# The opening of a two-block forward pass: modulation by matmul on four column groups, x loaded first, projections by halves

## The chip, the cores and the metric

The kernel runs on one core of one Trainium2 chip. The metric is device time in microseconds (us) for one launch; the kernel before takes 1517.32 us, the median of three runs (1516.11 to 1517.71). All data are fp32.

## The reference

The whole program is two transformer-like blocks on 512 tokens of width 1024. This case touches the start of the first one:

```python
mod_l = (silu(c)     @ w_mod + b_mod)[:, None, :]    # w_mod 1024 x 6144; 6 parts of 1024
mod_c =  silu(c_ctx) @ w_mod + b_mod                 # only csh1 and csc1 are used
sh1, sc1, g1, sh2, sc2, g2 = split(mod_l, 6)
csh1, csc1, ...            = split(mod_c, 6)
h  = rms(x,   norm1_g) * (1 + sc1)  + sh1            # 512 tokens
hc = rms(ctx, norm1_g) * (1 + csc1) + csh1           # 256 context tokens
p, pc = h @ w_in, hc @ w_in                          # q (384), kv (256), k_pe (32), f (512), ga, gb (1024 each)
# then: low-rank q, k, v, attention of 8 heads, a Fourier branch, the merge with w_out,
# 16 experts, and a second block (recurrent unit, short convolution, feed-forward)
```

## The kernel before

Everything is stored with channels on the 128 partitions. x is eight tiles of 128 channels by 512 tokens (`x0`), ctx eight tiles by 256 tokens (`c0`). The projections are done at better than single-pass precision: a weight and an activation are each split into a rounded part and a remainder (`w_hi`, `w_lo`, `h_hi`, `h_lo`) and each product is three matmuls (`mm3`, L817 to L819). One weight block is 128 x 128 values, and its three matmuls stream 512 tokens (256 for ctx).

**The weight stream.** All weights come in chunks of 128 x 2048 values (1 MB) through a ring of four slots, `raw`. SP (SyncE) issues the loads in the order of `CHUNKS`, and each refill waits until the chunk four places earlier has been used. A chunk that is to be split is rounded on ACT (L1392, `w_hi`) and its remainder is taken on POOL (L746, `w_lo`); there are three slots of these. A chunk of w_mod is used directly. Before, the first eight chunks are those of sc1 and sh1 (`mod_a`), then come the chunks of `s1` (w_in and others), and the 16 chunks of the other four parts of w_mod (`mod_b`) stand behind chunks 9 to 17 of `s1`.

**The first modulation** (`mod_a`, before). Each chunk has two tiles of 128 outputs. The first tile is done on PE with the weights stationary and the two columns of silu(c), silu(c_ctx) moving (L842). The second tile is done by DVE for c (L1754, L1756: a product and seven multiply-adds of 128 x 128, `macc_x`) and by POOL for c_ctx (L783, L765), and PE sums these over partitions with a column of ones (L847). `mod_evac` (L1706) adds the bias.

**The norm.** ACT squares x and ctx (L1416, L1417), DVE sums the eight tiles (L1768), PE sums over partitions (L866, `columns`), DVE takes the inverse square root by Newton steps (L1734 to L1746), PE spreads the result over partitions (L873, `broadcast`). Then for each tile j: DVE multiplies (`pre`, L1794), ACT adds the shift and rounds (`h_hi`, L1402), DVE takes the remainder (`h_lo`, L1801), in two buffers. PE projects `cq` 0 and 1 together as the tiles of h appear, then `cq` 2, `ckv`, `kpe`, and then `f` 0 (the first tile of the Fourier branch), the sums of squares `ssq_c`, `f` 1, and so on.

**The order** on each engine is written out by hand. A plan (`make_plan`) gives each PSUM tile a bank, says what frees it, and counts the tiles (`tile_full`), by which ACT knows when to split the next weight chunk and SP when a chunk has been used.

**The second modulation** (`mod_b`, L1721 and L1723) runs on DVE beside PE's projections `ga`, `gb` and `four_o`: for each of 16 chunks a product and seven multiply-adds of 128 x 256 elements into `macc` in SBUF. PE sums each over partitions (L856), and between them DVE evacuates `four_o` (L1923, `gbf`).

## Time and profile before

| | us |
|---|---|
| median of three runs | 1517.32 |
| the profiled execution | 1515.58 |
| its span | 1513.8 |
| PE busy in the span | 1412.9 (93%) |
| DVE busy | 747.3 (49%) |
| first projection matmul starts | 81.85 |
| `f` 0 starts | 125.06 |

The profile page gives the busy time of each engine over the span and in 40 slices, the chain of work that ended last, and the costliest groups of instructions. Its slices show PE at 4 to 5 tenths in the first two, and at 9 nearly everywhere later. In a timeline row the columns are start, length, engine, line, operation, output and inputs, shape and count; what stands in brackets is the idle time before it and what ended that. On PE an fp32 matmul has two rows. PE rows overlap: what counts is the spacing of their starts.

### The profile page before, as it was taken

How to read it: one execution, taken by the hardware profiler on the slowest of the kernel's cores; microseconds unless marked ns; L12 is line 12 of the kernel's file. 1: busy time of each engine (PE TensorE's matmuls, PEld its weight loads, DVE VectorE, ACT ScalarE, POOL GpSimd, SP SyncE). 2: the span in 40 equal slices, each digit the busy share in tenths (PEclk: the TensorE clock that was granted, in tenths of full speed). 3: DMA queues.
4: the chain of work that ended last, by engine and by line, in shares of the span. 5: the costliest groups of instructions: out<-in, count | busy, mean ns of one | idle time of the engine just before them, and what ended most of it. 6: DMA issues, size and time to landing. Idle time of an engine off the chain costs nothing.

```text
span 1513.8 us, 15775 instructions
## 1 busy us (share of the span) xinstructions
PE 1412.9 (93%) x6456; PEld 1056.9 (70%) x6456; DVE 747.3 (49%) x1245; ACT 445.7 (29%) x563; POOL 423.6 (28%) x127
## 2 busy tenths in 40 slices
PE   5599999998999977999998999999999999999997
PEld 5478887775667874444443767877888888888886
DVE  7962479976567144333323475571145154352442
ACT  1141332224654131110001346332234143232330
POOL 6531233330211210000001322543424434344340
PEclk9998999998999968999999999999999999999998
DMA  7241116650012423999998311322213322223201
GB/s 275 108 167 56 57 56 255 247 221 0 30 54 84 167 111 147 397 385 399 399 396 343 116 56 56 111 87 80 84 63 132 111 84 94 83 102 111 84 1 56
DMA packets 31908, 221.96 MB, mean 147 GB/s; under 512 B 3776, under 2 KB 4416, under 8 KB 5472
## 3 DMA queue, kind: packets, MB, share of 16 engines
q1 hardware_dynamic: 30400, 215.77, 37.3%
q10 hardware_dynamic: 1440, 5.24, 0.9%
q8 instruction: 48, 0.79, 0.2%
q14 instruction: 20, 0.16, 0.0%
HBM read 218.90 MB, written 2.10 MB: 146 GB/s over the span
## 4 chain that ended last, share of the span: by engine, by line
PE 79%; DVE 17%; issue 1%; ACT 1%; DMA 1%; POOL 0%; DVEq 0%; SPq 0%; ACTq 0%
PE psum L817 18%; PE psum L818 18%; PE psum L819 18%; PE psum L1196 12%; DVE macc L1723 5%; DVE macc_x L1756 3%; PE psum L1068 2%; PE psum L866 2%; PE psum L1181 2%; PE psum L1156 1%; PE psum L1157 1%; DMA raw<-in_stream 1%; PE psum L1043 1%; PE psum L1125 1%; PE psum L1184 1%
## 5 line engine op out<-in xcount | busy, mean ns | idle before, releaser
L746 POOL TENSOR_TENSOR w_lo<-raw,w_hi 128x2048 fp32r<-128x2048 f32 x82 | 378.5, 4618 | 974.2 <-ACT w_hi L1392 699.6
L817 PE MATMUL psum<-b_hi,w_hi 128*128 128x512 f32 x608 | 239.8, 394 | 2.4 <-DVE conv_u L2171 1.3
L819 PE MATMUL psum<-b_hi,w_lo 128*128 128x512 f32 x608 | 236.7, 389 | 0.0
L818 PE MATMUL psum<-b_lo,w_hi 128*128 128x512 f32 x608 | 236.6, 389 | 0.0
L1392 ACT ACTIVATE w_hi<-raw 128x2048 fp32r<-128x2048 f32 x82 | 156.2, 1907 | 232.4 <-DMA raw<-in_stream 116.4
L817 PEld LDWEIGHTS psum<-b_hi,w_hi 128*128 128x128 f32 x608 | 114.2, 188 | 28.2 <-DVE conv_u L2171 2.2
L818 PEld LDWEIGHTS psum<-b_lo,w_hi 128*128 128x128 f32 x608 | 114.2, 188 | 24.2 <-issue 1.2
L819 PEld LDWEIGHTS psum<-b_hi,w_lo 128*128 128x128 f32 x608 | 114.1, 188 | 24.0
L1196 PE MATMUL psum<-ex,xe 128*64 128x512 f32 x512 | 122.3, 602 | 0.7 <-ACT xe L1574 0.7
L2015 DVE SCALAR_TENSOR_TENSOR x<-psum,mod,x 128x512 f32<-128x512 f32 x72 | 53.9, 750 | 128.4 <-PE psum L1184 91.0
L2013 DVE TENSOR_TENSOR x<-psum,x 128x512 f32<-128x512 f32 x40 | 27.6, 692 | 159.9 <-PE psum L819 159.9
L817 PE MATMUL psum<-h_hi,w_hi 128*128 128x512 f32 (+1 forms) x208 | 84.0, 404 | 5.0 <-DVE h_lo L1801 1.8
L1723 DVE SCALAR_TENSOR_TENSOR macc<-raw,small,macc 128x256 f32<-128x256 f32 x112 | 84.1, 751 | 4.0
L818 PE MATMUL psum<-h_lo,w_hi 128*128 128x512 f32 (+1 forms) x208 | 82.3, 396 | 0.0
L819 PE MATMUL psum<-h_hi,w_lo 128*128 128x512 f32 (+1 forms) x208 | 82.3, 396 | 0.0
L1196 PEld LDWEIGHTS psum<-ex,xe 128*64 128x64 f32 x512 | 32.2, 136 | 62.1 <-issue 61.3
L817 PE MATMUL psum<-ff_hi,w_hi 128*128 128x512 f32 x192 | 75.3, 392 | 0.0
L819 PE MATMUL psum<-ff_hi,w_lo 128*128 128x512 f32 x192 | 74.8, 389 | 0.0
L818 PE MATMUL psum<-ff_lo,w_hi 128*128 128x512 f32 x192 | 74.7, 389 | 0.0
L2242 DVE TENSOR_TENSOR psum<-psum,rstd_s 128x512 f32<-128x512 f32 x48 | 33.5, 697 | 77.4 <-PE psum L819 77.4
L1196 PE MATMUL psum<-ex,act_e 128*64 128x512 f32 x256 | 58.4, 610 | 1.6 <-DVE act_e L2142 1.6
L817 PEld LDWEIGHTS psum<-h_hi,w_hi 128*128 128x128 f32 (+1 forms) x208 | 39.3, 189 | 15.8 <-issue 2.9
(352 smaller groups left out, 2422.4 us busy)
## 6 DMA issues: line engine op xcount, KB each, us to landing
raw<-in_stream SPq DMA_DIRECT2D x106, 1024.0 KB, 4.9
ex<-in_stream SPq DMA_DIRECT2D x96, 1024.0 KB, 8.9
x<-in_x SPq DMA_DIRECT2D x1, 2048.0 KB, 15.4
x<-in_x ACTq DMA_DIRECT2D x1, 2048.0 KB, 7.4
out<-y_out ACTq DMA_DIRECT2D x8, 256.0 KB, 2.2
c<-in_ctx SPq DMA_DIRECT2D x1, 1024.0 KB, 17.5
wab<-in_wab ACTq DMA_DIRECT2D x1, 1024.0 KB, 6.7
cols<-in_cols SPq DMA_DIRECT2D x1, 166.5 KB, 2.3
```

The lines of the kernel that those rows point to most:

```text
L746: nc.gpsimd.tensor_tensor(w_lo[:, slot, :], raw[:, raw_slot, :], w_hi[:, slot, :].bitcast(F32), ALU.subtract).then_inc(w_lo_done, 1)
L817: mm(o, w[0], x[0], start=start, stop=False)
L818: mm(o, w[0], x[1], start=False, stop=False)
L819: return mm(o, w[1], x[0], start=False, stop=stop)
L866: last = mm(o[:, at + t:at + t + 1], src[:, t * P:(t + 1) * P], one[0:rows, :], start=start and t == 0, stop=stop, skip_group_check=True)
L1068: return mm(psum[:, 6 + h % 2, :], va, probs[:, k % 3, :], start=k == 0, stop=k == KT - 1)
L1196: last = mm(o[e * CAP:(e + 1) * CAP, :], x_of(k, e), w[:, (2 * (k - k0) + e) * T:(2 * (k - k0) + e + 1) * T], start=k == 0, stop=k == ks - 1)
L1392: A(w_hi[:, c % NHL, :], raw[:, n % NRAW, :], ACT.Copy).then_inc(w_hi_done, 1)
L1723: ins = V.scalar_tensor_tensor(out=acc, in0=w[:, :, k, :], scalar=csil[:, 2 * k:2 * k + 1], in1=acc, op0=ALU.mult, op1=ALU.add)
L1756: ins = V.scalar_tensor_tensor(out=macc_x[:, c, :], in0=w, scalar=s, in1=macc_x[:, c, :], op0=ALU.mult, op1=ALU.add)
L2015: ins = V.scalar_tensor_tensor(out=x1[:, j, :], in0=o, scalar=scale, in1=x1[:, j, :], op0=ALU.mult, op1=ALU.add)
L2242: V.tensor_tensor(o, o, rstd, ALU.mult).then_inc(ffz_done, 1)
```

## The change

1. **Order of loads.** cols, then x in four pieces of two tiles each with semaphores of their own, ident, then the ring. The stream is now: chunk 0 of `s1`, two chunks of w_mod, chunk 1 of `s1`, six chunks of w_mod, chunk 2 of `s1`. ctx is loaded just ahead of ring chunk 10.
2. **First modulation.** The chunks of w_mod are laid out by rows: each holds four blocks of 128 inputs by 512 outputs. They are now the moving operand, and silu(c), silu(c_ctx), padded with zeros to 32 columns (`cpad`), the stationary one. The four blocks go to four groups of 32 columns of the array and so to four groups of 32 partitions of one PSUM bank, two chunks summed in each. ACT copies the 128 x 512 result to SBUF (`mod_rows`), and four small matmuls with a 0/1 matrix (`sel`) sum the four groups and turn the result back to channels on partitions (`mod_tile`). The four tiles hold the first half of sc1, the first half of sh1, the second half of sc1, the second half of sh1. DVE's and POOL's part in it is gone.
3. **Norm of x.** PE sums the squares of all eight tiles itself (`ssq_x`, 32 small matmuls); the norm of ctx has its own tile (`ssq_cc`) and Newton steps, and its squares and DVE sum stand between the halves.
4. **Projections by halves.** The five tiles `cq` 0 to 2 and `ckv` 0, 1 of x are open together. For h tiles 0 to 3 all five take each tile as it comes, with modulation tiles 2 and 3 between them; then each of the five takes h tiles 4 to 7. The weight blocks are laid out to match: chunk 0 has `cq` for tiles 0 to 3, chunk 1 has `ckv`, chunk 2 `cq` for tiles 4 to 7, `kpe` and the start of `f`.
5. **Second modulation.** The accumulator lies in PSUM bank 7; only the last multiply-add writes `macc` in SBUF.

```diff
+MOD_M0 = (8, 0, 12, 4)
+MOD_BEHIND = {0: 2, 1: 6, 9: 1, 10: 2, 11: 2, 12: 2, 13: 2, 14: 2, 15: 2, 16: 2, 17: 1}
...
+    p.add("ssq_x", by=("rcol_done", 1), bank=5)
     for g in range(4):
-        if g == 3:
-            p.add("ssq_xc", by=("rcol_done", 1))
-        p.add("mod", g, raw=(2 * g, 2 * g + 1))
-    p.add("bc_x", by=("pre_done", KD))
-    p.add("bc_c", by=("pre_done", 2 * KD))
+        p.add("rows", g, by="act", raw=(2 * g, 2 * g + 1), bank=6)
+        if g == 0:
+            p.add("bc_x", by=("pre_done", KD), bank=5)
+        p.add("mod", g, bank=7)
+    p.add("ssq_cc", by=("rcol_done", 2), bank=6)
     for j in range(QL):
-        p.add("cq", j, split=blocks(s1, S1_QKV + j * 8 * B, 8))
+        p.add("cq", j, split=(s1, s1 + 2), bank=j)
+    p.add("bc_c", by=("pre_done", 2 * KD), bank=7)
     for j in range(KL):
-        p.add("ckv", j, 0)
-        p.add("ckv", j, 1, split=blocks(s1, S1_QKV + (QL + j) * 8 * B, 8))
-    p.add("kpe", 0)
+        p.add("ckv", j, 0, split=(s1 + 1,), bank=QL + j)
+    p.add("kpe", 0, split=blocks(s1, S1_KPE, 2), bank=5)
...
+            for i in range(4):
+                sp.dma_start(x0[:, 2 * i:2 * i + 2, :], x_d[:, 2 * i:2 * i + 2, :]).then_inc(x_in[i], 16)
+            sp.dma_start(ident[:], ident_d).then_inc(ident_in, 16)
             for n in range(NRAW):
                 load(n, n)
-            sp.dma_start(x0[:], x_d).then_inc(x_in, 16)
-            sp.dma_start(c0[:], ctx_d).then_inc(x_in, 16)
-            sp.dma_start(ident[:], ident_d).then_inc(consts_in, 16)
...
+                if n == 10:
+                    sp.dma_start(c0[:], ctx_d).then_inc(ctx_in, 16)
                 refill(n)
...
+            def mod_rows_tile(g):
+                o = open_tile("rows", g)
+                for c in range(2):
+                    w = raw_chunk(RAW_OF_RAW[2 * g + c])
+                    for i in range(4):
+                        last = mm(o[32 * i:32 * i + 32, :], cpad[:, 4 * c + i, :], w[:, i * T:(i + 1) * T],
+                                  start=c == 0, stop=c == 1)
+                done(last)
...
                 o = open_tile("mod", g)
-                for c in range(2):
-                    w = raw_chunk(2 * g + c)
-                    for k in range(KD):
-                        mm(o[:, 4 * c:4 * c + 2], w[:, k * B:(k + 1) * B], csil[:, 2 * k:2 * k + 2],
-                           start=k == 0 and c == 0, stop=k == KD - 1, skip_group_check=True)
-                for c in range(2):
-                    for i, (acc, ready) in enumerate(((macc_x, macc_x_done), (macc_c, macc_c_done))):
-                        pe.wait_ge(ready, 2 * g + c + 1)
-                        last = mm(o[:, 4 * c + 2 + i:4 * c + 3 + i], acc[:, 2 * g + c, :], one, start=False, stop=True,
-                                  skip_group_check=True)
+                pe.wait_ge(freed_act, PLAN.freed_count(TILE["rows", g]))
+                for b in range(4):
+                    last = mm(o[:, 2 * b:2 * b + 2], mod_rows[:, g % 2, b * P:(b + 1) * P], col("sel", 0, 2),
+                              start=True, stop=True)
                 done(last)
...
+            o = open_tile("ssq_x")
+            for j in range(KD):
+                pe.wait_ge(sq_done, j // 2 + 1)
+                last = columns(o, 0, sq_x0[:, j, :], TT, start=j == 0, stop=j == KD - 1)
+            done(last)
             pe.wait_ge(silu_done, 1)
-            for g in range(4):
-                if g == 3:
-                    o = open_tile("ssq_xc")
-                    pe.wait_ge(sum_done, 1)
-                    columns(o, 0, sum_x, TT)
-                    pe.wait_ge(sum_done, 2)
-                    done(columns(o, TT, sum_c, 2, start=False))
-                mod_tile(g)
-            pe.wait_ge(consts_in, 16 * 7)
-            o, o2 = open_tile("bc_x"), open_tile("bc_c")
+            mod_rows_tile(0)
+            pe.wait_ge(ident_in, 16)
+            o = open_tile("bc_x")
             wait_rcol()
             done(broadcast(o, 0, TT))
-            done(broadcast(o2, TT, 2))
+            mod_tile(0)
+            mod_rows_tile(1)
+            mod_tile(1)
...
+            for k in range(4):
+                for i in range(QL + KL):
+                    qkv_step(i, k)
+                if k == 0:
+                    mod_rows_tile(2)
+                if k == 1:
+                    mod_tile(2)
+                    mod_rows_tile(3)
+                if k == 2:
+                    mod_tile(3)
+            o = open_tile("ssq_cc")
+            pe.wait_ge(sum_done, 1)
+            done(columns(o, 0, sum_c, 2))
+            for i in range(QL + KL):
+                if i == QL:
+                    o = open_tile("bc_c")
+                    wait_rcol()
+                    done(broadcast(o, 0, 2))
+                for k in range(4, KD):
+                    last = qkv_step(i, k)
+                done(last)
+            pe.wait_ge(consts_in, 16 * 6)
...
+            def rows_copy(g):
+                o = take("rows", g)
+                if g >= 2:
+                    full(act, "mod", g - 2)
+                A(mod_rows[:, g % 2, :], o, ACT.Copy).then_inc(freed_act, 1)
+            def h_hi_part(j):
+                hi_of_pre(h_hi[:, j, :], pre[:, j % 2, :], bias=mod[:, j, 0:1])
+            rows_copy(0)
+            rows_copy(1)
+            for j in range(2):
+                h_hi_part(j)
+            rows_copy(2)
+            for j in range(2, 4):
+                h_hi_part(j)
+            rows_copy(3)
+            act.wait_ge(ctx_in, 16)
             A(sq_c0[:], c0[:], ACT.Square).then_inc(sq_done, 1)
-            act.wait_ge(consts_in, 16 * 7)
-            A(dftc_hi[:], dftc[:], ACT.Copy).then_inc(act_seq, 1)
-            for g in range(4):
-                split_weights(TILE["mod", g])
-            for j in range(KD):
-                hi_of_pre(h_hi[:, j, :], pre[:, j % 2, :], bias=mod[:, j, 0:1])
+            for j in range(4, KD):
+                h_hi_part(j)
             for j in range(KD):
                 hi_of_pre(hc_hi[:, j, :], pre[:, j % 2, 0:TC], bias=mod[:, j, 1:2])
+            act.wait_ge(consts_in, 16 * 6)
+            A(dftc_hi[:], dftc[:], ACT.Copy).then_inc(act_seq, 1)
...
                 dve.wait_ge(raw_full[n % NRAW], 16 * (n // NRAW + 1))
+                if c < 2:
+                    dve.wait_ge(qtok_done, 2 * TT)
+                else:
+                    dve.wait_ge(macc_done, c - 1)
                 w = raw[:, n % NRAW, :].rearrange("p (m k c) -> p m k c", m=2, k=KD)
-                acc = macc[:, c % 4, :, :]
+                acc = psum[:, 7, c % 2 * 2 * B:(c % 2 + 1) * 2 * B].rearrange("p (m c) -> p m c", m=2)
                 link(V.tensor_scalar(acc, w[:, :, 0, :], csil[:, 0:1], None, ALU.mult))
                 for k in range(1, KD):
-                    ins = V.scalar_tensor_tensor(out=acc, in0=w[:, :, k, :], scalar=csil[:, 2 * k:2 * k + 1], in1=acc,
-                                                 op0=ALU.mult, op1=ALU.add)
+                    ins = V.scalar_tensor_tensor(out=acc if k < KD - 1 else macc[:, c % 4, :, :], in0=w[:, :, k, :],
+                                                 scalar=csil[:, 2 * k:2 * k + 1], in1=acc, op0=ALU.mult, op1=ALU.add)
...
+            inverse_norms(take("ssq_x"), 4, [(0, 4, 1.0 / D)])
+            mod_evac(0)
+            gains(0)
+            mod_evac(1)
+            norm(4, mk0(x0, a1, take("bc_x"), "h"), lo0(h_lo, h_hi, 0, "h", T))
+            dve.wait_ge(sq_done, 5)
+            V.tensor_reduce(sum_c[:], sq_c0[:].rearrange("p k t -> p t k"), AX.X, ALU.add).then_inc(sum_done, 1)
+            mod_evac(2)
+            gains(1)
+            mod_evac(3)
+            norm(KD, mk0(x0, a1, bank("bc_x"), "h"), lo0(h_lo, h_hi, 0, "h", T), 4)
+            inverse_norms(take("ssq_cc"), 2, [(0, 2, 1.0 / D)])
+            norm(KD, mk0(c0, a1c, take("bc_c")[:, 0:TC], "hc"), lo0(hc_lo, hc_hi, 1, "hc", TC))
```

How the instructions move on PE at the start (before; `macc_x` and `macc_c` are the partial products of DVE and POOL, `small` holds the norms):

```order
L842 MATMUL psum<-small,raw 128x2 x16
L847 MATMUL psum<-ones,macc_x 128x1
L847 MATMUL psum<-ones,macc_c 128x1
...
L866 MATMUL psum<-ones,sum_x 128x1 x4
L866 MATMUL psum<-ones,sum_c 128x1 x2
L842 MATMUL psum<-small,raw 128x2 x16
...
L873 MATMUL psum<-ident,small 128x128 x6
L817 MATMUL psum<-h_hi,w_hi 128x512
```

and after:

```order
L854 MATMUL psum<-ones,sq_x_67 128x1 x32
L826 MATMUL psum<-raw,cpad 32x512 x8
L861 MATMUL psum<-ident,small 128x128 x4
L835 MATMUL psum<-cols,mod_rows 128x2 x4
L826 MATMUL psum<-raw,cpad 32x512 x8
L835 MATMUL psum<-cols,mod_rows 128x2 x4
L802 MATMUL psum<-h_hi,w_hi 128x512
```

The first projection now stands behind two of the four modulation tiles; the other two (L826, L835) stand behind the projections of h tiles 0, 1 and 2.

On ACT, after the change, from the squares of x to the shift of the last tile of h (`w_hi` is the splitting of weight chunks):

```order
L1433 ACTIVATE sq_x_67<-x_65 128x1024 x4
L1406 ACTIVATE w_hi<-raw 128x2048 x2
L1440 ACTIVATE mod_rows<-psum 128x512 x2
L1416 ACTIVATE h_hi<-pre,mod 128x512 x2
L1440 ACTIVATE mod_rows<-psum 128x512
L1416 ACTIVATE h_hi<-pre,mod 128x512 x2
L1406 ACTIVATE w_hi<-raw 128x2048
L1440 ACTIVATE mod_rows<-psum 128x512
L1454 ACTIVATE sq_c_68<-c_66 128x2048
L1416 ACTIVATE h_hi<-pre,mod 128x512 x4
```

Before, both squares stood ahead of the two `w_hi`, and nothing stood between the eight `h_hi`; now the third weight chunk, the copy of a modulation tile and the squares of ctx stand in their middle.

On DVE, after the change, between tile 3 and tile 4 of h:

```order
L1810 SCALAR_TENSOR_TENSOR h_lo<-pre,mod,h_hi 128x512 x2
L1825 TENSOR_REDUCE sum_c<-sq_c_68 128x256
L1743 TENSOR_TENSOR mod<-psum,cols 128x8
L1816 SCALAR_TENSOR_TENSOR small<-mod,cols 128x4 x2
L1743 TENSOR_TENSOR mod<-psum,cols 128x8
L1803 SCALAR_TENSOR_TENSOR pre<-x_65,small,psum 128x512 x2
```

The sum of the squares of ctx now stands ahead of the evacuation of modulation tile 2, which frees the bank of modulation tile 3.

## Rows read from the trace of the kernel before

**Rows 1.** Busy time by stretch: length; PE, PEld, DVE, ACT, POOL busy; PEclk; DMA share, GB/s.

```profile
0.00:81.80 81.80, 41.16 (x184) 40.07 (x184) 69.13 (x90) 12.42 (x9) 44.23 (x39) 1.00 0.52 200
81.80:125.00 43.20, 43.15 (x216) 34.84 (x217) 21.43 (x37) 17.73 (x25) 13.82 (x3) 1.00 0.33 127
205.00:335.00 130.00, 123.77 (x564) 101.59 (x563) 117.18 (x215) 30.00 (x31) 46.72 (x10) 0.99 0.56 212
280.00:285.00 5.00, 5.00 (x16) 3.92 (x16) 4.82 (x6) 2.40 (x2) 2.89 (x1) 0.66 0.87 351
```

**Rows 2.** The chain that ended last, 0 to 84 us: shares by line.

```profile
by line: DVE macc_x L1756 54.7%; issue 9.8%; DVE macc_x L1754 9.1%; DMA raw<-in_stream 6.1%; DVE sum_c L1768 4.4%; PE psum L873 2.5%; PE psum L847 2.4%; PE psum L817 1.4%; DVE sum_x L1768 1.4%; PE psum L818 1.0%; DVE h_lo L1801 0.9%; DVE pr
```

**Rows 3.** Timeline, the start: loads and what waited for them.

```profile
3.28 0.47 SPq L694 DMA_DIRECT2D x<-in_x  x1
6.41 2.02 DVE L1754 TENSOR_SCALAR macc_x<-raw,small 128x128 f32<-128x128 f32 x1 [5.54 <-DMA raw<-in_stream]
21.28 3.62 ACT L1416 ACTIVATE sq_x<-x 128x4096 f32<-128x4096 f32 x1 [17.99 <-DMA c<-in_ctx]
```

**Rows 4.** DMA issues of the page: KB each, us to landing.

```profile
raw<-in_stream SPq DMA_DIRECT2D x106, 1024.0 KB, 4.9
```

**Rows 5.** Timeline: small matmuls and Newton's end, start of the span to 80 us.

```profile
36.11 6.96 PE L842 MATMUL psum<-small,raw 128*128 128x2 f32 x32
77.14 2.90 PE L873 MATMUL psum<-ident,small 128*128 128x128 f32 x12 [1.40 <-DVE mod L1706]
```

**Rows 6.** Timeline: expert matmuls, two groups of 64 columns, moving 512 columns.

```profile
606.96 5.37 PE L1196 MATMUL psum<-ex,act_e 128*64 128x512 f32 x24
```

**Rows 7.** Timeline of PE: the first projections, later ones, and ctx, kpe and f.

```profile
81.85 0.76 PE L817 MATMUL psum<-h_hi,w_hi 128*128 128x512 f32 x1 [1.81 <-DVE h_lo L1801]
82.83 0.63 PE L819 MATMUL psum<-h_hi,w_lo 128*128 128x512 f32 x1
83.26 0.63 PE L817 MATMUL psum<-h_hi,w_hi 128*128 128x512 f32 x1
...
105.14 0.39 PE L818 MATMUL psum<-h_lo,w_hi 128*128 128x512 f32 x1
105.36 0.39 PE L819 MATMUL psum<-h_hi,w_lo 128*128 128x512 f32 x1
...
116.68 0.28 PE L819 MATMUL psum<-hc_hi,w_lo 128*128 128x256 f32 x1
116.80 0.39 PE L817 MATMUL psum<-h_hi,w_hi 128*32 128x512 f32 x1
117.03 0.39 PE L818 MATMUL psum<-h_lo,w_hi 128*32 128x512 f32 x1
...
125.06 0.40 PE L817 MATMUL psum<-h_hi,w_hi 128*128 128x512 f32 x1
```

**Rows 8.** Timeline: weight splitting, the sum of ctx, steps of h.

```profile
58.29 1.91 ACT L1392 ACTIVATE w_hi<-raw 128x2048 fp32r<-128x2048 f32 x1 [31.28 <-DMA raw<-in_stream]
58.37 3.72 DVE L1768 TENSOR_REDUCE sum_c<-sq_c 128x256 f32<-128x2048 f32 x1
60.27 9.01 POOL L746 TENSOR_TENSOR w_lo<-raw,w_hi 128x2048 fp32r<-128x2048 f32 x2 [9.70 <-ACT w_hi L1392]
83.85 0.72 ACT L1402 ACTIVATE h_hi<-pre,mod 128x512 fp32r<-128x512 f32 x1 [0.72 <-DVE pre L1794]
85.18 0.75 DVE L1801 SCALAR_TENSOR_TENSOR h_lo<-pre,mod,h_hi 128x512 fp32r<-128x512 f32 x1
```

**Rows 9.** Second modulation on DVE, with POOL working (230 to 239) and not (226).

```profile
226.81 3.61 DVE L1723 SCALAR_TENSOR_TENSOR macc<-raw,small,macc 128x256 f32<-128x256 f32 x7
230.72 7.82 DVE L1723 SCALAR_TENSOR_TENSOR macc<-raw,small,macc 128x256 f32<-128x256 f32 x7
233.45 4.81 POOL L746 TENSOR_TENSOR w_lo<-raw,w_hi 128x2048 fp32r<-128x2048 f32 x1 [16.00 <-ACT w_hi L1392]
```

**Rows 10.** DVE and POOL around 309 us.

```profile
308.35 4.61 POOL L746 TENSOR_TENSOR w_lo<-raw,w_hi 128x2048 fp32r<-128x2048 f32 x1 [8.79 <-ACT w_hi L1392]
308.85 0.69 DVE L1923 TENSOR_TENSOR gbf<-psum,sg 128x512 f32<-128x512 f32 x1 [2.88 <-ACT sg L1470]
309.52 3.58 DVE L1721 TENSOR_SCALAR macc<-raw,small 128x256 f32<-128x256 f32 x1
```

More of the change, by code:

```diff
@@ L155, in raw_chunks @@
             if name == "s1":
-                for _ in range(MODB_BEHIND.get(c, 0)):
+                for _ in range(MOD_BEHIND.get(c, 0)):
                     add(False)
@@ L1432, in _ @@
                 square(sq_q[:, j, :], take("cq", j))
-            for j in range(KL):
-                square(sq_kv[:, j, 0:T], take("ckv", j, 0))
-                square(sq_kv[:, j, T:TK], take("ckv", j, 1)[:, 0:TC])
-            A(sqk[NOPE:QK, 0:T], take("kpe", 0)[0:ROPE, :], ACT.Square).then_inc(act_seq, 1)
-            A(sqk[NOPE:QK, T:TK], take("kpe", 1)[0:ROPE, 0:TC], ACT.Square).then_inc(act_seq, 1)
+            for s in range(2):
+                w = slice(T, TK) if s else slice(0, T)
+                n = TC if s else T
+                for j in range(KL):
+                    square(sq_kv[:, j, w], take("ckv", j, s)[:, 0:n])
+                A(sqk[NOPE:QK, w], take("kpe", s)[0:ROPE, 0:n], ACT.Square).then_inc(act_seq, 1)
             hi(f_hi[:, 0, :], take("f", 0))
@@ L1704, in mod_evac @@
             def mod_evac(g):
-                b = cols[:, COLS["b_mod"] + 4 * g:COLS["b_mod"] + 4 * g + 4].unsqueeze(2).to_broadcast([P, 4, 2])
-                free(V.tensor_tensor(mod[:, 4 * g:4 * g + 4, :], take("mod", g)[:, 0:8].rearrange("p (m c) -> p m c", c=2),
+                m = MOD_M0[g]
+                b = col("b_mod", m, 4).unsqueeze(2).to_broadcast([P, 4, 2])
+                free(V.tensor_tensor(mod[:, m:m + 4, :], take("mod", g)[:, 0:8].rearrange("p (m c) -> p m c", c=2),
                                      b, ALU.add))
@@ L1803, in lo0, with gains @@
                 return f
-            norm(KD, None, mk0(x0, a1, take("bc_x"), "h"), lo0(h_lo, h_hi, 0, "h", T))
-            norm(KD, None, mk0(c0, a1c, take("bc_c")[:, 0:TC], "hc"), lo0(hc_lo, hc_hi, 1, "hc", TC))
-            nsq = 2
+            def gains(half):
+                for i, a in ((0, a1), (1, a1c)):
+                    link(V.scalar_tensor_tensor(out=a[:, 4 * half:4 * half + 4], in0=mod[:, KD + 4 * half:KD + 4 * half + 4, i],
+                                                scalar=1.0, in1=col("norm1_g", 4 * half, 4), op0=ALU.add, op1=ALU.mult))
+            inverse_norms(take("ssq_x"), 4, [(0, 4, 1.0 / D)])
[11 more added lines that the diff above has]
+            norm(KD, mk0(c0, a1c, take("bc_c")[:, 0:TC], "hc"), lo0(hc_lo, hc_hi, 1, "hc", TC))
+            dve.wait_ge(act_seq, 1)
+            link(V.tensor_tensor(dftc_lo[:], dftc[:], dftc_hi[:].bitcast(F32), ALU.subtract))
+            nsq = 5
             for j in range(QL):
@@ L2322 @@
     w_mod = a["w_mod"][0]
-    mod = tiles(w_mod)
+    rows_a = [w_mod[(4 * c + i) * P:(4 * c + i + 1) * P, m * P:m * P + T] for m in MOD_M0 for c in range(2) for i in range(4)]
+    mod = np.concatenate(rows_a + [tiles(w_mod)[:, 8 * CH:]], axis=1)
     w_in = a["w_in"][0]
```

143 lines of the change are left out of this document (52 added, 91 removed), and 2 rows, old and new, of the table _n.

## The prediction

> **What bounds the kernel now.** I read the busy time by stretch first. PE is busy 41 of the first 81.8 us and practically all of the next 43 [rows 1]; the page has it at nine tenths nearly everywhere after. So what ends PE's early waits shortens the program, and what is done beside PE later is free. The chain of waits says who sets the opening: 54.7% of it is DVE's multiply-add for the first modulation, 9.1% its product, and 4.4% the sum of ctx's squares [rows 2]. PE's first projection starts at 81.85, released by the first tile of h, and `f` 0, which both kernels reach with the same work done, starts at 125.06 [rows 7]. Between 205 and 335 us PE is idle 130 − 123.8 = 6.2 us, and in one stretch of 5 us its granted clock is 0.66 [rows 1], 1.7 us more; this is the stretch of the second modulation, on a DVE busy 117 of 130 us. The reader is to see two places only: the start, and this one.
>
> **The opening, step by step.** *Loads.* The first ring chunk is there at 6.41, after cols and itself (1.2 MB); ctx, the last large load, at 21.3 after 7.5 MB [rows 3]. That is 6.3 MB in 14.9 us, 0.42 MB a us, 2.5 us a chunk. With x first: first piece of x near 5, all of x at 8.9, then chunk 0 of `s1` 11.5, two of w_mod 14.0 and 16.5, chunk 1 of `s1` 19.0.
>
> *PE, squares of x.* `ssq_x` is 32 small matmuls, 64 rows. 32 rows of small matmuls (moving 2 columns) took 6.96 us in the same opening [rows 5], so 13.9 us: from 6.2 (one ACT square after the first piece) to 20.1. This is new on PE and now sets the start; Newton's steps and `bc_x` lie beside or just behind it.
>
> *Rows tiles.* The trace has no matmul on four groups of 32 columns. The nearest row is the experts': two groups of 64 columns, 512 moving, 24 rows in 5.37 us [rows 6], so 0.224 a row; two matmuls side by side are four rows, 0.9 us. One alone would be 0.9 as well if the pair is really side by side. Bounds for a chunk of four: 0.9 us (all side by side) and 3.6 (one after the other). I take 0.9, since the experts' rows show groups overlapping. The first projections start 0.43 us apart (82.83, 83.26) and later ones 0.22 [rows 7]: after the opening's small matmuls and waits PE works at the lower of its two clock levels (1.2 against 2.4 GHz), though the page's granted clock stands at 1.00. I take the slow rate for this opening too: 1.7 us a chunk. Rows tile 0: 20.1 to 23.5. `bc_x` is 8 rows of the kind of which 12 took 2.90 [rows 5], 1.9 us, and modulation tile 0 8 rows at 0.22, 1.7 us: to 27.2.
>
> *The ring.* The second chunk of rows tile 1 takes the slot of the first w_mod chunk, so it is loaded when rows tile 0 is done, 23.5, and lands 4.9 us later [rows 4] at 28.4. Its matmuls end at 30.1, ACT's copy (like `h_hi`, 0.72 [rows 8]) at 30.8, modulation tile 1 at 32.6, its evacuation at 32.8, and from `pre` to the first projection the chain before needs 2.5 us (`pre`, `h_hi`, `h_lo`; 0.75, 0.72, 0.75 [rows 8]). First projection at 35.4 instead of 81.85: 46.4 us earlier.
>
> *From there to `f` 0.* The projections are the same matmuls, 43.2 us before (125.06 − 81.85, the slow start included). Added on PE: rows tiles 2 and 3 at the full clock, 3.6; modulation tiles 2 and 3, 2.9; `ssq_cc` 0.6 and `bc_c` 1.0. Then a new wait. PE reaches modulation tile 3 at 35.4 + 5.0 + 1.8 + 3.4 + 1.2 + 1.8 + 3.4 = 52.0 (three groups of 15 matmuls, the rows tiles, tile 2). Its bank is freed by DVE's evacuation of tile 2, queued behind the sum of ctx's squares, 3.72 us [rows 8], which waits for ACT's square (1.9 us), which stands behind the third weight chunk: loaded at 42.2 when rows tile 2 is done, landed 47.1, split by ACT in 1.91 [rows 8]. That gives copy 49.7, square 51.6, sum 55.3, evacuation 55.5: PE waits 3.5 us. The row of 280 to 285 us shows the clock granted at 0.66 after a wait of this size [rows 1], so I add 1.7 us. At tile 7 of h PE is ahead of DVE by 1.2 us. Sum of what is added: 3.6 + 2.9 + 1.6 + 3.5 + 1.7 + 1.2 = 14.5. `f` 0 starts at 35.4 + 43.2 + 14.5 = 93.1, **32.0 us earlier**.
>
> *Covers.* The norm of ctx (8 steps on DVE, under 8 us) ends near 81, its matmuls start near 84; weight chunk 3 is split by ACT and POOL (1.91 and 4.6 us [rows 8]) by 90, `f` 0 needs it at 93. Each has some 3 us; if one fails, the wait is a few us.
>
> A rule that speaks against the change: the Trainium skill (TensorEngine Tiling, Key Properties) says that changing the tiling mode drains TensorE, and the rows tiles change it eight times. The trace goes from 128 to 32 output columns at 116.68 and the next rows start 0.12 and 0.23 us on [rows 7], no later than within one mode. By the row the sum stands; what a drain would cost is a rival below.
>
> **The second modulation.** A chunk's seven multiply-adds take DVE 3.61 us, or 7.82 when POOL splits a weight chunk beside them [rows 9]: one of them lasts as long as POOL's. Ten POOL operations fall in this stretch [rows 1], each worth 4.2 us of DVE. A DVE operation with one input in PSUM ran through POOL's at 0.69 us (308.85), while a product with only SBUF operands, 0.6 us later, was held for 3.58 [rows 10]. With the accumulator in PSUM the multiply-adds are of the first kind: 16 chunks at 3.9 us are 63 us instead of about 100, and PE's projections (5.4 us and more for each) set the pace. What PE can get back is 6.2 + 1.7 = 7.9 us. Bounds: 0 (POOL holds the new form too, or PE finds another wait) and 7.9. I take **7.0**, since nearly all of PE's waits there hang on DVE or on the ring that DVE feeds.
>
> The first operation of a chunk has one SBUF input and writes PSUM, and no row shows that form. By the row at 309.52 it can be held; the Trainium skill (VectorE: DVE Perf Modes, Mode 2×_2P) has the held mode only with source and destination both in SBUF, so it would never be. It is one operation in eight, so the sum goes by the rest either way.
>
> After 335 us nothing is moved: the same waits come 39 us earlier.
>
> **Sum.** The profiled execution took 1515.58 us: 1515.6 − 32.0 − 7.0 = 1476.6. The median of the three runs is 1.7 above it, so 1478.3, **1478 us**.
>
> **Rivals.**
> - *Column groups one after the other.* For: no row shows four. Against: the experts' pairs overlap [rows 6]. Rows tile 0 would cost 13.4 instead of 3.4 (eight at 1.68), the second chunk of rows tile 1 5 more, tiles 2 and 3 5.4 more each: 26 us, so 1504.
> - *The second modulation gives nothing*, by either bound above: 1485.
> - *PE's clock is high in the opening.* Small matmuls at half the time: `ssq_x` 7 us less, though the ring then holds rows tile 1 for a while; no slow stretch after the wait: 8 us less in all, 1470. Against: 6.96 us of small matmuls in a row did not speed up [rows 5].
> - *Each change between 128 and 32 columns stops PE.* Eight changes (into and out of four rows tiles), each at most as long as one slow fp32 matmul, 1.7 us: 13 us, 1491. Against: the spacing at 116.68 [rows 7]. This is the case of the Trainium skill's rule above (TensorEngine Tiling).
> - *The gain is lost altogether* by a wait in the coupled queues (ring, ACT, DVE, PE in order) that I have missed: 1517. It would need 39 us in a stretch of 90.
> - *Slower: the accumulator in PSUM makes DVE the bound.* Place: the 16 chunks, DVE from 222 to 326 us before. It decides when a chunk takes more than (326 + 32 − 222 − 5)/16 = 8.2 us, that is 1.0 us an operation instead of 0.5. At 1.5 us the chunks end near 222 + 192 + 5 = 419, 93 us later than now, less 32: 1578. Against: 0.69 us for 512 elements with PSUM input [rows 10]; these have 256.
>
> **Chances.** Forecast 0.62; groups in turn 0.12; stops at mode changes 0.03; no gain in the second modulation 0.09; high clock 0.10; all lost 0.02; slower 0.02. A difference under 0.2%, 3 us, can't be told from none. Faster 0.96, the same 0.02, slower 0.02. Range 1469 to 1497: the high-clock case and a few single misses (a cover of 3 us gone, the slow clock kept longer, part of the groups in turn) are in it, the full 26 us and the last two are not.
>
> **What would show it.** Right: `f` 0 near 93 us, first projection near 35; `ssq_x` about 14 us; a rows tile 2 us or less when dense; PE waiting 3 to 4 us for DVE in the middle of the halves; no multiply-add over 1 us beside POOL's; PE idle under 2 us in the stretch of `ga`, `gb`, `four_o`. Wrong: rows tiles of 7 us; a multiply-add held by POOL; `ctx` or weight chunk 3 releasing PE late.

## The result and the profile after

The changed kernel takes 1473.18 us (median of four runs, 1472.33 to 1475.54) where the kernel before took 1516.71 beside it: ratio 0.9721 [0.9698, 0.9744]. The forecast was 1478 with a range of 1469 to 1497. Run again later, with the kernel before beside it once more, it took 1474.46 (five runs) against 1516.45, ratio 0.9728 [0.9708, 0.9748]. Its profiled execution took 1472.33 us with a span of 1470.5: 43.3 us under that of before, where the prediction's sum said 39.0.

First the busy time by stretch, with the columns of [rows 1]; the first two lines end at the first projection and at `f` 0, the third is the stretch of the second modulation, the rest are short looks at the clock.

```profile
0.00:35.40 35.40, 22.97 (x120) 18.11 (x120) 6.29 (x20) 12.22 (x13) 9.70 (x8) 0.95 0.92 338
35.40:91.50 56.10, 53.13 (x272) 40.54 (x273) 28.18 (x55) 20.53 (x29) 9.45 (x3) 0.91 0.41 155
171.50:297.00 125.50, 124.41 (x577) 103.08 (x577) 89.89 (x215) 31.65 (x32) 46.07 (x10) 1.00 0.60 226
...
55.00:61.00 6.00, 5.69 (x18) 4.82 (x19) 4.30 (x10) 2.00 (x3) 0.00 (x0) 0.55 0.51 201
61.00:64.00 3.00, 3.00 (x14) 2.50 (x13) 2.64 (x7) 0.84 (x2) 0.00 (x0) 0.77 0.00 0
```

PE was idle 40.6 us before the first projection and is now idle 12.4. In the third stretch it was idle 6.2 of 130 us and is now idle 1.1 of 125.5.

The chain that ended last, 0 to 92 us, shares by line, answers to [rows 2]:

```profile
by line: PE psum L854 15.3%; PE psum L802 15.0%; PE psum L803 14.1%; PE psum L804 13.8%; DMA raw<-in_stream 10.4%; PE psum L826 7.2%; DMA x<-in_x 5.2%; DVE sum_c L1825 4.0%; PE psum L835 3.4%; issue 2.8%; ACT sq_c L1454 2.0%; ACT mod_rows L
```

DVE's multiply-adds, 54.7% of it before, are gone; the squares on PE (L854) are the largest line, and a tenth is the ring.

The timeline of PE and of what it waits for, from the squares of x to `f` 0:

```profile
7.14 13.78 PE L854 MATMUL psum<-ones,sq_x 128*128 128x1 f32 x64 [7.14 <-ACT sq_x L1433]
20.86 3.64 PE L826 MATMUL psum<-raw,cpad 128*32 128x512 f32 x16
24.43 1.35 PE L861 MATMUL psum<-ident,small 128*128 128x128 f32 x8
25.61 0.95 PE L835 MATMUL psum<-cols,mod_rows 128*128 128x2 f32 x8
26.49 1.06 PE L826 MATMUL psum<-raw,cpad 128*32 128x512 f32 x8
29.41 1.06 PE L826 MATMUL psum<-raw,cpad 128*32 128x512 f32 x8 [1.86 <-DMA raw<-in_stream]
31.29 1.49 PE L835 MATMUL psum<-cols,mod_rows 128*128 128x2 f32 x8 [0.81 <-ACT mod_rows L1440]
35.44 0.79 PE L802 MATMUL psum<-h_hi,w_hi 128*128 128x512 f32 x1 [2.66 <-DVE h_lo L1810]
...
40.48 1.92 PE L826 MATMUL psum<-raw,cpad 128*32 128x512 f32 x16
42.33 0.50 PE L802 MATMUL psum<-h_hi,w_hi 128*128 128x512 f32 x1
...
51.50 3.68 DVE L1825 TENSOR_REDUCE sum_c<-sq_c 128x256 f32<-128x2048 f32 x1 [6.37 <-ACT sq_c L1454]
55.31 1.66 PE L835 MATMUL psum<-cols,mod_rows 128*128 128x2 f32 x8 [2.94 <-DVE mod L1743]
...
91.53 0.40 PE L802 MATMUL psum<-h_hi,w_hi 128*128 128x512 f32 x1
```

These answer to [rows 5] and [rows 7]. The first projection stands at 35.44 (81.85 before), `f` 0 at 91.53 (125.06): 33.5 us earlier. The sum of ctx's squares runs from 51.50 to 55.18, and PE waits behind it.

Two executions of one and the same opening are not alike. The opening of before, unchanged in the first experiment below, starts its projections at 81.85 in one trace and at 77.97 in the other, and `f` 0 at 125.06 and 122.08. The changed opening, up to its first projection the same in four traces of this record, starts them between 34.64 and 36.56, and in the three of them that are the same up to `f` 0 this stands between 90.42 and 93.06. No run shows what makes this scatter. A difference of two single traces carries some 3 us of it.

The summary of DVE's operations of the second modulation (shortest, median, longest duration in ns; first and last start), first before, then after, answers to [rows 9]:

```profile
L1723 DVE SCALAR_TENSOR_TENSOR macc<-raw,small,macc x112: 483/485/4940, 222.9 to 325.1; 128x256 f32<-128x256 f32 x112
```

```profile
L1764 DVE SCALAR_TENSOR_TENSOR psum<-raw,small,psum x96: 487/490/493, 189.0 to 276.1; 128x256 f32<-128x256 f32 x96
L1764 DVE SCALAR_TENSOR_TENSOR macc<-raw,small,psum x16: 481/481/482, 192.1 to 276.6; 128x256 f32<-128x256 f32 x16
L1762 DVE TENSOR_SCALAR psum<-raw,small x16: 475/486/489, 188.4 to 272.9; 128x256 f32<-128x256 f32 x16
```

The longest fell from 4940 to 493 ns: none is held beside POOL any more, though POOL works as long as before (46.07 us in the stretch, 46.72 before). The 16 products and 112 multiply-adds together take DVE 62.5 us instead of 92.9; the prediction had 63 and about 100.

Where the 43.3 us came from, by the start of the same work in both traces: `f` 0 33.5 us earlier, the transposes of q behind the second modulation 42.0 (350.6 and 308.6), the first expert matmul 41.0, the last matmul of the feed-forward 43.2. So in this pair of traces the opening gave 33.5 and the stretch with the second modulation 8.5; everything later changed the distance by at most 2.2 us.

### The profile page after: what moved, and what is told of

Same layout as the page of the kernel before. It is cut to its first block, busy times and chain, and to the rows that moved or that the text cites. A ratio compares the mean times of both kernels' runs of the same rounds, so it can differ in the third digit from the quotient of the medians.

```text
span 1470.5 us, 15704 instructions
## 1 busy us (share of the span) xinstructions
PE 1400.3 (95%) x6448; PEld 1039.3 (71%) x6448; DVE 661.9 (45%) x1194; ACT 448.9 (31%) x571; POOL 388.8 (26%) x96
## 4 chain that ended last, share of the span: by engine, by line
PE 88%; DVE 8%; ACT 1%; DMA 1%; issue 1%; POOL 0%; DVEq 0%; SPq 0%; ACTq 0%
PE psum L802 20%; PE psum L804 20%; PE psum L803 20%; PE psum L1210 12%; PE psum L854 3%; PE psum L1082 2%; PE psum L1195 2%; PE psum L1170 1%; PE psum L1171 1%; PE psum L1057 1%; DMA raw<-in_stream 1%; PE psum L1139 1%; PE psum L1198 1%; PE psum L1269 1%; PE psum L861 1%
## 5 line engine op out<-in xcount | busy, mean ns | idle before, releaser
L803 PEld LDWEIGHTS psum<-b_lo,w_hi 128*128 128x128 f32 x608 | 114.2, 188 | 24.5 <-issue 1.2
L802 PE MATMUL psum<-h_hi,w_hi 128*128 128x512 f32 (+1 forms) x208 | 85.3, 410 | 3.7 <-DVE h_lo L1810 2.7
L2267 DVE TENSOR_TENSOR psum<-psum,rstd_s 128x512 f32<-128x512 f32 x48 | 33.5, 698 | 77.4 <-PE psum L804 77.4
L1764 DVE SCALAR_TENSOR_TENSOR psum<-raw,small,psum 128x256 f32<-128x256 f32 x96 | 47.0, 490 | 3.4
```

The source lines that it names most:

```text
L802: mm(o, w[0], x[0], start=start, stop=False)
L803: mm(o, w[0], x[1], start=False, stop=False)
L1764: ins = V.scalar_tensor_tensor(out=acc if k < KD - 1 else macc[:, c % 4, :, :], in0=w[:, :, k, :], scalar=csil[:, 2 * k:2 * k + 1], in1=ac ...
L2267: V.tensor_tensor(o, o, rstd, ALU.mult).then_inc(ffz_done, 1)
```

## The experiments

Each starts from the kernel named; the cuts show the lines that matter. `f` 0 is its start in the profiled execution. The experiments ran in groups, each with the kernel before beside it, whose median was between 1513.58 and 1516.71 us. Ratios to it are the safer comparison between groups.

**Which part gives what.** The kernel before with the accumulator in PSUM alone:

```diff
-acc = macc[:, c % 4, :, :]
+acc = psum[:, 7, c % 2 * 2 * B:(c % 2 + 1) * 2 * B]...     # the last multiply-add still writes macc
```

The waits for the bank, which the diff of the change shows, come with it.

> The kernel before, with only the second modulation's accumulator moved to PSUM bank 7; the opening is the old one. Theory: POOL's weight splitting holds a DVE operation with two SBUF inputs and not one with an input in PSUM, and this alone gives what the changed kernel gained behind f 0, about 8.5 us: 1508 us (1506 to 1511), every multiply-add near 0.49 us, PE idle under 2 us between 205 and 335 us and no fall of its clock there. Rival: that stretch gained because the opening shifted the ring of weights against POOL; PSUM alone gives 0 to 3 us: 1514 to 1517.

Measured: 1506.35 us (8 runs; before 1513.58, 13 runs), ratio 0.9945 [0.9925, 0.9965], 7.2 us by the medians: as the theory said, and outside the rival's 1514 to 1517. The stretch of [rows 1]:

```profile
205.00:335.00 130.00, 129.24 (x599) 107.18 (x598) 93.74 (x225) 35.48 (x39) 46.07 (x10) 1.00 0.55 210
```

PE's idle time is 0.8 us instead of 6.2, and no slow clock is left. From `f` 0 (122.08) to the transposes of q (339.9) it takes 217.8 us, before 225.5: 7.7 us.

The changed kernel with the accumulator back in SBUF:

```diff
-out=acc if k < KD - 1 else macc[:, c % 4, :, :]            # acc in psum bank 7
+out=acc                                                    # acc = macc[:, c % 4, :, :]
```

> The changed kernel with the second modulation's accumulator back in SBUF. Theory: the opening alone is worth 33.5 us (f 0 at 91.5 instead of 125.1) and the two parts add up: 1481 us (1479 to 1484), with multiply-adds of 4 to 5 us beside POOL's operations again. Rival (the new ring order frees that stretch by itself): 1473 to 1476.

Measured: 1482.11 us (4 runs), ratio 0.979 [0.9766, 0.9813]: 31.5 us under the kernel before, inside the theory's range and outside the rival's. The hold is back, and with it PE's waits (waits of PE, 160 to 336 us: total, times, longest us):

```profile
L1760 DVE SCALAR_TENSOR_TENSOR macc<-raw,small,macc x112: 483/485/4922, 190.1 to 292.7; 128x256 f32<-128x256 f32 x112
```

```profile
PE psum L802 <- DVE gbf L1944: 3.8, 2, 1.9
...
PE psum L802 <- DVE mod L1749: 1.6, 1, 1.6
```

The two ratios multiplied give 0.9736, against 0.9721 and 0.9728 measured for both parts together: the parts add up within their intervals, so neither hides the other. By medians the opening is worth 31.5 us; the 33.5 of the two traces above holds some of the scatter.

**Are the four column groups side by side?** The changed kernel with all four blocks on one group of 32 columns, the same number of matmuls:

```diff
-last = mm(o[32 * i:32 * i + 32, :], cpad[:, 4 * c + i, :], ..., start=c == 0, stop=c == 1)
+last = mm(o[0:32, :], cpad[:, 4 * c + i, :], ..., start=c == 0 and i == 0, stop=c == 1 and i == 3)
```

The copy and the small matmuls then take 32 partitions.

> The changed kernel with the four blocks of a w_mod chunk on one group of 32 columns, so one after the other into the same 32 partitions; copy and small matmuls take 32 partitions. Theory: the four groups really run side by side, so a chunk takes 3.6 us instead of 1.0 at the full clock, and the four rows tiles lengthen PE's path by 14 to 22 us: 1487 to 1495. Rival: the short time of a chunk comes from the narrow stationary operand (32 columns to load), not from the groups: 1473 and chunks near 1.0 us.

Measured: 1492.28 us (4 runs), ratio 0.9861 [0.9839, 0.9883]: 19 us slower than the changed kernel by medians, 21 by the ratios, inside the theory's range.

```profile
20.87 8.51 PE L826 MATMUL psum<-raw,cpad 128*32 128x512 f32 x16
...
48.75 7.05 PE L826 MATMUL psum<-raw,cpad 128*32 128x512 f32 x16
```

At the high clock a rows tile takes 7.05 us on one group and 1.92 on four: 3.7 times. The prediction's rival "one after the other" is excluded, and so is this run's own, that the narrow stationary operand and not the groups makes the chunk short: it is as narrow here.

**The wait behind the sum of ctx's squares.** ACT's square and DVE's sum moved behind the last four tiles of h:

```diff
 # DVE
 norm(4, mk0(x0, ...), ...)
-dve.wait_ge(sq_done, 5); V.tensor_reduce(sum_c[:], ...)
 mod_evac(2); gains(1); mod_evac(3)
 norm(KD, mk0(x0, ...), ..., 4)
+dve.wait_ge(sq_done, 5); V.tensor_reduce(sum_c[:], ...)
 # ACT: the square likewise; PE: ssq_cc three projection tiles later, bc_c one
```

> The changed kernel with the square and the sum of ctx moved behind tiles 4 to 7 of h on ACT and DVE, and its norm's matmuls one and two projection tiles later. Theory: PE's wait of 2.9 us for modulation tile 3 and the slow clock behind it (granted 0.5 from 56 to about 61 us) go together, and the norm of ctx is still in time for its matmuls: 5 to 7 us less, 1466 to 1468. Rival: the ctx chain is then late (its matmuls wait for the last hc tile, or f 0 for the fourth weight chunk), and it is 1471 to 1475. If the wait goes and the slow clock stays: 1470.

Measured: 1469.93 us (5 runs, 1466.52 to 1473.09), ratio 0.9704 [0.9682, 0.9726]. That is between the theory's 1466 to 1468 and the rival's 1471 to 1475. The third case, a slow clock without the wait, has the time right but not the reason, since PE no longer waits for modulation tile 3 and the clock stays up (timeline, and busy time by stretch):

```profile
52.09 0.95 PE L836 MATMUL psum<-cols,mod_rows 128*128 128x2 f32 x8
...
58.58 0.51 PE L803 MATMUL psum<-h_hi,w_hi 128*128 128x512 f32 x1 [0.48 <-DVE h_lo L1812]
...
78.58 0.36 PE L803 MATMUL psum<-hc_hi,w_hi 128*128 128x256 f32 x1 [0.73 <-DVE cqg L1843]
```

```profile
56.00:60.00 4.00, 3.52 (x14) 2.19 (x13) 3.24 (x5) 2.83 (x3) 0.00 (x0) 1.00 0.52 217
```

`f` 0 starts at 87.14, 4.4 us earlier than in the changed kernel. So the wait cost 2.9 us by itself, and the slow clock behind it more: modulation tile 3 and the 15 matmuls after it take 7.63 us in the changed kernel and 4.35 here, 3.3 us less. Some 2 us go again later, at the two new short waits (0.48 for the last tile of h, 0.73 for ctx) and the starts behind them. Of the whole time 3.3 us arrived by the medians, 2.6 by the ratios, with ranges that overlap; the profiled execution of this kernel (1472.38) shows one place where such a gain goes. The transposes of q are still 4.3 us earlier and the first expert matmul 3.1. Then come the same expert matmuls behind the same gap of 0.78 us, first in the changed kernel, then in this one:

```profile
788.40 7.09 PE L1210 MATMUL psum<-ex,act_e 128*64 128x512 f32 x32 [0.78 <-DVE act_e L2167]
```

```profile
785.20 8.78 PE L1212 MATMUL psum<-ex,act_e 128*64 128x512 f32 x32 [0.78 <-DVE act_e L2169]
```

1.7 us go in one clock fall, which one execution has and the other not: from 787 to 789 us the granted clock is 0.50 here and 1.00 there.

**x in pieces.** One load for x, and all four squares wait for it:

```diff
-sp.dma_start(x0[:, 2 * i:2 * i + 2, :], ...).then_inc(x_in[i], 16)     # i = 0 to 3
+sp.dma_start(x0[:], x_d).then_inc(x_in[0], 16)
```

> The changed kernel with x loaded in one piece, still first. Theory: the squares' matmuls (13.8 us on PE) set the start and now begin about 5.3 us later, near 12.4 us; every later link (slot release, second chunk of rows tile 1, first projection) moves with them: f 0 near 96.8, 1478 us (1476 to 1480). Rival: the loads, which are saturated until 22 us, set the first projection anyway and the pieces are worth nothing: 1473 to 1475.

Measured: 1477.81 us (4 runs), ratio 0.9746 [0.9725, 0.9767]. The time is in the theory's range, and the rival, that the pieces are worth nothing, falls. The theory's step was too long, though: it had the squares at 12.4 and `f` 0 at 96.8. The squares start at 10.21 instead of 7.14, the first projection at 38.88, `f` 0 at 94.94, 3.4 us later than in the changed kernel and 1.9 later than in the latest of the three traces with x in pieces. The reason is that one load of x lands sooner than four pieces do. ACT's squares, first in the changed kernel, whose last piece comes at 11.3 us, then here, where all of x is there at 9.0:

```profile
5.95 1.06 ACT L1433 ACTIVATE sq_x<-x 128x1024 f32<-128x1024 f32 x1 [2.50 <-DMA x<-in_x]
...
11.32 1.06 ACT L1433 ACTIVATE sq_x<-x 128x1024 f32<-128x1024 f32 x1 [0.23 <-DMA x<-in_x]
```

```profile
9.01 3.89 ACT L1434 ACTIVATE sq_x<-x 128x1024 f32<-128x1024 f32 x4 [5.56 <-DMA x<-in_x]
```

The pieces pay because the first comes 3.1 us earlier and PE has 13.8 us of squares to do behind it.

**Two modulation tiles behind the first projections.** All four put ahead of them on PE:

```diff
+for g in range(2, 4):
+    mod_rows_tile(g); mod_tile(g)
 ...
-if k == 0: mod_rows_tile(2)      # and so on, between the projections of h tiles 0 to 3
```

> The changed kernel with all four modulation tiles ahead of the first projection on PE; ACT, DVE and loads as they are. Theory: the halves hide the second half's weights, ctx and its sum behind 20 us of projections; without them the first projection waits for modulation tile 3, near 54 us instead of 35, and f 0 comes 10 to 13 us later, since PE's wait in the middle and the tiles' matmuls there go: 1483 to 1487. Rival: PE's work is what counts and the order is worth only the wait for loads, 2 to 4 us: 1475 to 1477.

Measured: 1480.97 us (4 runs), ratio 0.9769 [0.9745, 0.9792]: between the theory's 1483 to 1487 and the rival's 1475 to 1477, so the order is worth 7 to 8 us. The first projection starts at 54.66, as the theory had it, since modulation tile 3 still waits for DVE, 11.4 us now:

```profile
52.93 1.87 PE L835 MATMUL psum<-cols,mod_rows 128*128 128x2 f32 x8 [11.38 <-DVE mod L1739]
```

But `f` 0 is only 7.1 us later than in the changed kernel, and the theory had 10 to 13. DVE has made the first four tiles of h by 38.4 us and makes the other four from 55.1 to 61.2, ahead of PE, so the projections run to `f` 0 without a stop.

**The 13.8 us of squares on PE.** DVE adds the squares in pairs, so PE takes half as many:

```diff
+for i in range(4):
+    dve.wait_ge(sq_done, i + 1)
+    V.tensor_tensor(sq_x0[:, 2 * i, :], sq_x0[:, 2 * i, :], sq_x0[:, 2 * i + 1, :], ALU.add).then_inc(sum_done, 1)
```

> The changed kernel with the squares of x added in pairs on DVE (four adds of 128 x 512), so PE has 16 instead of 32 small matmuls for them. Theory: PE's squares end near 15 instead of 20.9 us; rows tile 0 then waits for its weights (near 19.5), the second chunk of rows tile 1 for the loads, which are saturated: first projection near 33.5 instead of 35.4, and the time 1.5 to 3 us less, 1470 to 1472. Rival (PE's squares alone set the start, not the loads): 6 us less, 1467. If the release of slots by chunk 0 of s1 binds: no change.

Measured: 1473.08 us (5 runs), ratio 0.9715 [0.9697, 0.9733]. The theory (1470 to 1472, first projection near 33.5) and the rival (1467) both fail, and the third case, no change, has the time. The squares end at 15.3 instead of 20.9, and nothing comes of it:

```profile
16.02 1.93 PE L826 MATMUL psum<-raw,cpad 128*32 128x512 f32 x8 [0.71 <-DMA raw<-in_stream]
...
23.68 1.87 PE L835 MATMUL psum<-cols,mod_rows 128*128 128x2 f32 x8 [2.33 <-ACT mod_rows L1442]
...
27.99 1.93 PE L826 MATMUL psum<-raw,cpad 128*32 128x512 f32 x8 [0.47 <-DMA raw<-in_stream]
...
35.22 0.80 PE L802 MATMUL psum<-h_hi,w_hi 128*128 128x512 f32 x1 [2.66 <-DVE h_lo L1812]
```

The rows tiles now wait for their loads, and modulation tile 0 for ACT's copy, which stands behind the splitting of a weight chunk. The load that rows tile 0 releases is issued 4.2 us earlier than in the changed kernel and takes longer to land, since it now runs behind the load of the chunk before it, issued at 19.95 when POOL has split chunk 0 of `s1`. From the chain that ended last, first the changed kernel, then this one:

```profile
24.56 4.81 DMA raw<-in_stream
```

```profile
20.34 7.60 DMA raw<-in_stream
```

So its matmuls start at 27.99 instead of 29.41, only 1.4 us earlier. Of these 1.4 us the clock takes 1.2: with the waits between its steps PE works at the low level, so that chunk and modulation tile 1 take 1.93 and 1.84 us where the changed kernel has 1.06 and 1.49. The prediction's "now sets the start" holds for the squares only together with the loads: both end within a us or two of each other.

**Both edits together.** Pairs, and the late square of ctx:

> The pairs on DVE and the late ctx together. The kernel with the late ctx alone had f 0 at 87.2 instead of 91.5 us. Theory: the two add up: f 0 near 85.3, 1467 to 1468 us. Rival: the ctx chain (square, sum, norm, its squares, fourth weight chunk) binds once the rest is early, and f 0 stays at 87.

Measured: 1468.29 us (5 runs), ratio 0.9688 [0.967, 0.9706], the first projection at 34.19 and `f` 0 at 86.69. The theory had 85.3, the rival 87; the kernel with the late square alone had 87.14 and 1469.93 us. So the pairs add nothing that can be told from the scatter here either. To separate this from the changed kernel, both ran again side by side on one chip:

> The changed kernel itself, beside the next two on one chip and in the same rounds. Theory (the late context square takes 4.4 us off the first row tile of f, and only a clock fall at an expert gap hid it in the whole time): 1471 to 1474 us, 3 to 5 us above the kernel with pairs and the late context square. Rival (what the opening gives is given back later, whatever the state of the clock): within 1 us of it.

> Squares of x in pairs and the context square behind the h tiles 4 to 7, run again beside the changed kernel. Theory: f 0 at 86 to 87, 1467 to 1470 us, 3 to 5 us under the changed kernel. Rival (the gain is lost later): f 0 as early, but the whole time within 1 us of it.

Measured: the changed kernel 1474.46 (1473.54 to 1474.72), this one 1469.09 (1466.28 to 1469.73), five runs each that do not overlap, `f` 0 at 90.4 and 87.3. 3.1 us of the 5.4 are there by `f` 0, and at the transposes of q the two traces are 4.8 us apart (309.2 and 304.4). The rival, that it is all lost later, falls. The difference is a little above the 3 to 5 us expected; where the rest comes from is open. The `f` 0 of the four traces with the late square (86.7 to 87.9, with the kernel of the next paragraph) and of the four without it (the changed kernel twice, with the accumulator in SBUF, and with pairs alone: 90.4 to 93.1) do not overlap.

**Loads and the split on ACT.** The same, with the first four loads of w_mod ahead of the second chunk of `s1`, and that chunk's split behind ACT's copy of rows tile 1:

```diff
-MOD_BEHIND = {0: 2, 1: 6, ...}
+MOD_BEHIND = {0: 4, 1: 4, ...}
+SPLIT_DUE[1] = TILE["rows", 1] + 1
```

> The kernel with pairs and the late context square, and two more edits: the modulation weights of chunks 0 to 3 are loaded ahead of the second small load, and the split of chunk 1 on ScalarE stands behind the copy of rows tile 1. Theory (behind the squares, the order of loads and ScalarE's place for that copy bind the rows tiles): first projection at 30.5 to 31.5 instead of 34.2, f 0 near 83, about 1465 us. Rival (the first projection's other inputs, its weights' split and the second half of chunk 0, come at 33 to 34 whatever the rows tiles do): first projection at 33 to 34.5, f 0 at 86 to 87, 1467 to 1470 us.

Measured: 1467.21 us (5 runs, 1466.49 to 1471.9), ratio 0.9691 [0.9667, 0.9714], the first projection at 35.05 and `f` 0 at 87.87: no different from the one before (34.19 and 35.33, 86.69 and 87.31 in its two traces). The time is the rival's, but its reason is not the right one either. The rows tiles did come earlier, and DVE was ready:

```profile
27.31 1.84 PE L837 MATMUL psum<-cols,mod_rows 128*128 128x2 f32 x8 [0.81 <-ACT mod_rows L1445]
...
29.46 1.41 DVE L1809 SCALAR_TENSOR_TENSOR pre<-x,small,psum 128x512 f32<-128x512 f32 x2
29.95 4.50 POOL L762 TENSOR_TENSOR w_lo<-raw,w_hi 128x2048 fp32r<-128x2048 f32 x1 [10.02 <-ACT w_hi L1411]
...
31.00 4.00 DVE L1816 SCALAR_TENSOR_TENSOR h_lo<-pre,mod,h_hi 128x512 fp32r<-128x512 f32 x1
35.05 0.79 PE L804 MATMUL psum<-h_hi,w_hi 128*128 128x512 f32 x1 [5.91 <-DVE h_lo L1816]
```

The first `h_lo` takes 4.00 us instead of 0.75: all its operands lie in SBUF, and it ends at 35.00, 0.55 us after POOL's splitting of the moved chunk (34.45). `pre`, with one input in PSUM, runs through the same POOL operation at its usual rate. Moving the split out of ACT's way put POOL's part of it onto the one DVE operation that PE was waiting for; the 3.2 us it costs are about what the loads had won (modulation tile 1 at 27.31, in the two traces of the kernel before this one at 29.69 and 30.83). No run here moves the split once more to win them.

## Why the prediction was right

**The opening up to the first projection**: 35.4 predicted, 35.44 measured. Squares 13.9 against 13.78; rows tile 0 done at 23.5 against 24.5; the second chunk of rows tile 1 landed at 28.4 against 29.4. This us comes from the start: the squares began at 7.14 and not at 6.2. The last steps were shorter, since the clock had been up from about 25 us (1.06 for that chunk, not 1.7), and so two errors of 1 us cancelled. The agreement to 0.04 us is luck, as the 34.64 to 36.56 of the other traces show. The loads were mis-sized without harm: all of x was put at 8.9 us, and its last piece came at 11.3. The chain is as predicted, squares, rows tile 0, the load that it releases (PE waits 1.86 us for it), modulation tile 1; what was not seen is that the loads alone would hold the start nearly as late, which the pairs show.

**From there to `f` 0**: 43.2 + 14.5 = 57.7 predicted, 56.1 measured. The added 12.9 us are, by the rows: two rows tiles 3.8 (predicted 3.6), modulation tiles 1.8 (2.9: at the high clock one takes 0.9), `ssq_cc` and `bc_c` 1.0 (1.6), the wait for DVE 2.9 (3.5), the slow clock 3.4 (1.7: granted 0.55 for 6 us and 0.77 for 3), the wait at tile 7 of h none (1.2). The wait was found at its place, behind the sum of ctx's squares, which ended at 55.18 (55.3 predicted), and moving that sum took it away. The mis-sized term is the slow clock, taken from one row of before: it costs more than the wait that it follows, which is why one move gave 4.4 us for a wait of 2.9. It was put too low, and the modulation tiles, `ssq_cc`, `bc_c` and tile 7 of h too high, and the two cancelled in part. By medians the opening gave 31.5 us of the 32.0 predicted.

**The column groups**: the pair of [rows 6] carried over to four; 3.7 times, shown with one group. The rival's price was too high: groups in turn cost 19 us and not 26, so 1492, which the stated range would have held.

**Stops at mode changes**: The rows tile at 40.48 is followed by a 128-column matmul at 42.33, 1.85 us on for 16 rows, and `bc_x` follows rows tile 0 at 3.57 us without a gap. Around the rows tile at 40.48 two starts are 0.32 and 0.34 us apart instead of 0.23; the second of these 0.1 us stands behind `ssq_cc` too (63.30 to 63.61), which changes no group. Of the Trainium skill's rule that a change of tiling mode drains TensorE (TensorEngine Tiling, Key Properties), no more than that can be seen: the trace disagrees with a cost of 1.7 us a change.

**The second modulation**: 7.0 predicted, 8.5 in the profiled executions, 7.2 by medians with that edit alone. The 8.5 are above the prediction's own bound of 7.9, which was read from 205 to 335 us alone. PE's idle time between `f` 0 and the transposes of q fell from 10.9 to 5.1 us; the other 2.7 go with the granted clock, 0.97 and 0.98 in the mean of this stretch of some 220 us. The first operation of each chunk, which reads SBUF and writes PSUM, was left open between two answers. It was never held (475 to 489 ns). The Trainium skill has it so (VectorE: DVE Perf Modes, What auto-detection actually checks: the mode that uses both SBUF ports wants the source and the destination in SBUF), and the trace agrees. But unheld it takes 486 ns, where the form with both sides in SBUF had a median of 344:

```profile
L1721 DVE TENSOR_SCALAR macc<-raw,small x16: 337/344/3582, 222.5 to 321.6; 128x256 f32<-128x256 f32 x16
```

**The covers** of 3 us held: nothing between 64 and 91.5 us makes PE wait.

**The rivals.** Groups in turn: excluded. The high clock in the opening: a part of it came (up from about 25 us, not in the squares and rows tile 0, and down again behind the wait at 52). All lost: no. Slower: the multiply-adds took 0.49 us each, not 1.5.

## What to carry to other kernels

Sum an opening by walking all queues at once: the ring, ACT, PE and DVE each had a term within a us or two of being last, and halving the longest (the squares) gained nothing, in part because the waits that it opened kept the clock low. Price a short wait of TensorE together with the slow clock behind it. A multiply-add of DVE that must come in time should not stand beside a long operation of POOL with both its tensor inputs in SBUF; here one input in PSUM was enough to keep it free, and moving a POOL operation can create such a meeting. Before reading a gain of 1 to 3 us out of two traces, look how far two traces of one kernel are apart.
